# A two-layer-type transformer block pair on one Trainium2 core: both output projections cut into two halves of row blocks, the first half issued inside the attention

## The reference, cut to what matters

```python
# block 1
h = rms_norm(x, attn_pre_g)
q_a, k_a, v_a, q_b, k_b, v_b = split(h @ w_in)
y_a = rms_norm(swa_sink_attention(q_a, k_a, v_a, sinks, slopes), swa_out_g)     # 8 heads of 64, window 128
y_b = diff_attention(q_b, k_b, v_b, lam, slopes, subln_g, lambda_init)          # 4 heads of 2 x 64, values of 128
x = x + rms_norm(concat([y_a, y_b]) @ w_out, attn_post_g)
x = x + rms_norm(conv_ffn(rms_norm(x, ffn_pre_g), w_up, conv_w, conv_b, w_down), ffn_post_g)
# block 2: six modulation vectors from c, as shift, scale and gate
h = modulate(rms_norm(x, g_mix), shift_mix, scale_mix)
q_d, k_d, v_d, q_s, k_s, v_s = split(h @ w_in_2)
mixed = concat([rms_norm(dilated_mixture(q_d, k_d, v_d), g_dil_out),            # 8 heads of 64
                rms_norm(stick_breaking_attention(q_s, k_s, v_s), g_sb_out)])   # 8 heads of 64
x = x + gate_mix * (mixed @ w_out_2)
x = x + gate_ffn * hierarchical_moe(modulate(rms_norm(x, g_ffn), shift_ffn, scale_ffn))  # 32 experts, 2 of them per token
return rms_norm(x, g_final)
```

## Time and profile before

| what | us |
|---|---|
| median of 3 runs (lowest, highest) | 1098.78 (1098.1, 1101.7) |
| profiled execution, its own time | 1095.0 |
| its span, first to last instruction | 1093.2 |
| PE busy | 1016.3 (93%) |
| DVE busy | 538.4 (49%) |
| ACT busy | 330.3 (30%) |
| mean granted clock of TensorE | 0.97 |

### The profile page before, as it was taken

The page is one execution under the profiler, slowest core; times in us unless marked ns, Lnnn a source line. Parts: engine busy times, 40 slices in busy tenths (PEclk is TensorE's granted clock), DMA queues, the critical chain, the costliest instruction groups (busy, mean ns, idle before and its releaser), DMA issues.

```text
span 1093.2 us, 15144 instructions
## 1 busy us (share of the span) xinstructions
PE 1016.3 (93%) x5951; PEld 706.6 (65%) x5951; DVE 538.4 (49%) x901; ACT 330.3 (30%) x507; POOL 75.3 (7%) x109
## 2 busy tenths in 40 slices
PE   6798689999999999999988899999999999999995
PEld 5697569999899998889876444444444444433441
DVE  6756786988989996738674311111111011111113
ACT  4353645445445455527450100000000000000001
POOL 7200010110111110100010000000000000000000
PEclk9899689999999999899989999999999999999998
DMA  7315046778898864244345899799999999999991
GB/s 279 116 40 195 37 155 231 265 275 300 300 330 280 302 242 164 78 160 149 126 170 230 355 425 382 314 384 426 426 425 431 421 426 427 423 426 430 426 401 40
DMA packets 60366, 311.88 MB, mean 285 GB/s; under 512 B 4021, under 2 KB 5386, under 8 KB 47530
## 3 DMA queue, kind: packets, MB, share of 16 engines
q1 hardware_dynamic: 52464, 284.31, 66.1%
q0 software_dynamic: 7456, 26.91, 6.7%
q10 hardware_dynamic: 410, 0.16, 0.1%
HBM read 310.32 MB, written 1.05 MB: 285 GB/s over the span
## 4 chain that ended last, share of the span: by engine, by line
PE 78%; DVE 10%; DMA 5%; ACT 3%; issue 2%; SPq 0%; POOL 0%; DVEq 0%; POOLq 0%; ACTq 0%
PE bank L1134 10%; PE bank L1103 10%; PE bank L744 10%; PE bank L1094 10%; PE bank L745 10%; PE bank L746 10%; PE bank L1045 6%; PE bank L1058 5%; DVE ring_r L1516 5%; DMA ring<-in_w_up 3%; DMA ring<-in_w_in 2%; PE bank L829 1%; PE bank L798 1%; ACT ring_r L1203 1%; DMA final_g<-in_w_ada 1%
## 5 line engine op out<-in xcount | busy, mean ns | idle before, releaser
L744 PE MATMUL bank<-hT_r,ring_r 128*128 128x256 f32 x744 | 217.0, 292 | 11.9 <-DVE ring_r L1516 8.3
L746 PE MATMUL bank<-hT_r,ring_r 128*128 128x256 f32 x744 | 213.8, 287 | 0.0
L1516 DVE TENSOR_TENSOR ring_r<-ring,ring_r 128x2048 fp32r<-128x2048 f32 (+1 forms) x78 | 176.1, 2290 | 21.5 <-ACT ring_r L1203 21.0
L1203 ACT ACTIVATE ring_r<-ring 128x2048 fp32r<-128x2048 f32 (+1 forms) x78 | 144.1, 1891 | 46.0 <-DMA ring<-in_w_up 38.8
L744 PEld LDWEIGHTS bank<-hT_r,ring_r 128*128 128x128 f32 x744 | 146.4, 197 | 15.4 <-issue 9.9
L746 PEld LDWEIGHTS bank<-hT_r,ring_r 128*128 128x128 f32 x744 | 146.2, 197 | 0.0
L745 PE MATMUL bank<-v_tok_r,ring_r 128*128 128x256 f32 x512 | 145.5, 284 | 0.0
L1980 DVE TENSOR_TENSOR scratch<-scratch,bank 128x512 f32<-128x512 f32 x16 | 11.0, 687 | 237.0 <-PE bank L1103 237.0
L1103 PE MATMUL bank<-ring,scratch 128*64 128x512 f32 x496 | 113.3, 595 | 0.0
L1134 PE MATMUL bank<-ring,scratch 128*64 128x512 f32 x480 | 106.3, 595 | 6.6 <-ACT scratch L1417 6.6
L1094 PE MATMUL bank<-ring,scratch 128*64 128x512 f32 x480 | 105.6, 592 | 0.0
(11 more groups left out here) (292 smaller groups left out, 1417.8 us busy)
## 6 DMA issues: line engine op xcount, KB each, us to landing
ring<-in_w_up SPq DMA_DIRECT2D x47, 2048.0 KB, 12.6
ring<-in_w_down SPq DMA_DIRECT2D x37, 2048.0 KB, 10.3
ring<-in_w_gate SPq DMA_DIRECT2D x30, 2048.0 KB, 12.1
ring<-in_w_in SPq DMA_DIRECT2D x9, 2048.0 KB, 8.0
kT<-in_w_ada POOLq DMA_DIRECT2D x24, 512.0 KB, 9.1
ring<-in_w_out SPq DMA_DIRECT2D x4, 2048.0 KB, 8.3
scratch<-in_w_ada POOLq DMA_DIRECT2D x12, 512.0 KB, 6.5
final_g<-in_w_ada POOLq DMA_DIRECT2D x12, 512.0 KB, 7.1
```

Source lines behind the costliest of these rows:

```text
L744: pe.matmul(dst, lhs[0], rhs[0], start=start, stop=False, **flags)
L746: return pe.matmul(dst, lhs[1], rhs[0], start=False, stop=stop, **flags)
L1203: sc.activation(hi, raw, ACT.Copy).then_inc(s_whi, 1)
L1516: last = ve.tensor_tensor(lo, raw, hi, ALU.subtract)
```

## The change

- **First half of each output projection.** The heads that are done first (windowed in block 1, stick-breaking in block 2) fill one half of the concatenated rows: four of the eight row blocks. These rows are now scaled, transposed, split and multiplied during the attention of the other heads: FIRST_HALF gives the steps of PE (transposes in step 9 of block 1 and step 2 of block 2, the four results' first 12 matmuls each in steps 10 to 13 and 4 to 7), PARTS_AT those of ACT and DVE. The results stay in four PSUM banks (PROJ_BANKS), and `rest_of_projection` adds the other four row blocks behind the attention.
- **Splits.** In block 1 the first output chunk is split in steps 7 and 8 instead of 8 and 9, the second in steps 9 and 10 instead of behind the attention.
- **Projection items.** The last ten items of block 1 are ordered so that chunk 2 of w_in is used up earlier: the third and fourth query item come before the first value item.
- **Roots.** Norms of the two halves are asked for separately: two more powers on POOL in each block.
- **First loads.** SP issues chunks 1 and 2 of w_in ahead of the sinks and lambda vectors; ACT splits chunk 2 ahead of lambda's exponential and of its copies, and DVE takes the copies of items 1 and 3 ahead of the split of chunk 2.
- **Small ones.** The norm of the feed-forward part goes to another buffer (rows2), and POOL's first modulation loads wait for the transposes of that norm.

```diff
-        ROOTS += [(5 * t, 5) for t in range(T)]
+        ROOTS += [(5 * t, 1) for t in range(T)]
+        ROOTS += [(5 * t + 1, 4) for t in range(T)]
...
+        TURN_K = {"attn1": (0, KD), "swa": (0, HALF_K), "diff": (HALF_K, KD), "ffn": (0, KD), "attn2": (0, KD),
+                  "sb": (HALF_K, KD), "dil": (0, HALF_K), "moe": (0, KD)}
...
+        PROJ_BANKS = [{(0, 0): 6, (1, 0): 7, (0, 1): 0, (1, 1): 1}, {(0, 0): 4, (1, 0): 5, (0, 1): 0, (1, 1): 1}]
...
-        for pair_of in range(2):
-            for h in (2 * pair_of, 2 * pair_of + 1):
-                items1.append(((QB0 + h * P) // HALF, "q", ("pair", (QB0 + h * P) % HALF, 8 + 2 * h)))
-                items1.append(((KB0 + h * P) // HALF, "k", ((KB0 + h * P) % HALF, 1 + h)))
-            items1.append((3 + pair_of, "v", (S * (1 - pair_of), S, P + S * pair_of)))
...
+        items1 += [q_item(0), k_item(0), q_item(1), k_item(1), q_item(2), q_item(3), v_item(0), k_item(2), k_item(3),
+                   v_item(1)]
...
+        FIRST_HALF = [("swa", {9: None, 10: (0, 0), 11: (1, 0), 12: (0, 1), 13: (1, 1)}),
+                      ("sb", {2: None, 4: (0, 0), 5: (1, 0), 6: (0, 1), 7: (1, 1)})]
+        PARTS_AT = [(9, 10), (2, 3)]
...
-        SPLITS = [{1: (N_IN + 3, 0), 2: (N_IN + 3, 1), 4: (N_IN + 4, 0), 5: (N_IN + 4, 1), 8: (N_OUT, 0),
-                   9: (N_OUT, 1)},
+        SPLITS = [{1: (N_IN + 3, 0), 2: (N_IN + 3, 1), 4: (N_IN + 4, 0), 5: (N_IN + 4, 1), 7: (N_OUT, 0),
+                   8: (N_OUT, 1), 9: (N_OUT + 1, 0), 10: (N_OUT + 1, 1)},
...
+            for c in range(1, LANES):
+                straight(N_IN + c, w_in[:, :, c * HALF:(c + 1) * HALF])
             sp.dma_start(sinks, a["swa_sinks"][0].partition_broadcast(P)).then_inc(s_sink, 16)
             for n, name in enumerate(("diff_lq1", "diff_lk1", "diff_lq2", "diff_lk2")):
                 sp.dma_start(lamv[:, n, :], a[name][0].partition_broadcast(P)).then_inc(s_lamv, 16)
-            for c in range(1, IN_CHUNKS):
+            for c in range(LANES, IN_CHUNKS):
...
+                    tag, steps = FIRST_HALF[blk]
+                    if i in steps and steps[i] is None:
+                        if blk == 0:
+                            piece_taken(blk, len(items1))
+                        turn(tag, mix)
+                    elif i in steps:
+                        t, c = steps[i]
+                        if PROJ_BANKS[blk][t, c] < 2:
+                            pe.wait_ge(s_log[blk], len(units) - 1 + PROJ_BANKS[blk][t, c])
+                        out_projection(blk, tag, t, c, first=True)
+
+            def out_projection(blk, tag, t, c, first):
+                n = (N_OUT, N_OUT2)[blk] + c
+                split_ready(n)
+                w = split_view(n % LANES)
+                ks = range(*TURN_K[tag])
+                for j, k in enumerate(ks):
+                    pe.wait_ge(s_hT[tag], max(place_in_turn(tag, k) + 1, 2))
+                    last = product(PS[PROJ_BANKS[blk][t, c]][:, :], tiles(tag, k, t * P, P), both(w, k, 0, HALF),
+                                   start=(first and j == 0), stop=(not first and k == ks[-1]), skip_group_check=True)
+                return last
+
+            def rest_of_projection(blk, tag):
+                turn(tag, mix)
+                for t in range(T):
+                    for c in range(2):
+                        out_projection(blk, tag, t, c, first=False).then_inc(s_proj[blk], 1)
...
             split(N_IN + 1)
+            split(N_IN + 2)
             sc.wait_ge(s_lamx, 1)
             sc.activation(lam2, lam2, ACT.Exp).then_inc(s_lame, 1)
-            take(0, range(3))
-            split(N_IN + 2)
-            take(0, range(3, AHEAD[0]))
+            take(0, range(AHEAD[0]))
             softmaxes(0, BETWEEN[0], SPLITS[0])
-            split(N_OUT + 1)
-            rounded("mix1", lambda k: vec[:, 2, R_SWA + k:R_SWA + k + 1] if k < 4 else subc)
+            rounded("diff", gain_of_mix[0])
...
+                    if blk == 1 and i in (1, 2):
+                        stick_breaking_scale(i - 1)
+                    if blk == 0 and i - 4 in (ends[("swa", t)] for t in range(T)):
+                        scale_window(units[i - 4]["t"])
+                    if i == PARTS_AT[blk][1]:
+                        low(("swa", "sb")[blk], gain_of_mix[blk])
```

More of the change, by code:

```diff
@@ L834, in attention @@
                         project(blk, n_base, n)
-            def out_projection(blk, n_base):
-                tag = ("mix1", "mix2")[blk]
+                    tag, steps = FIRST_HALF[blk]
[20 more added lines that the diff above has]
+                turn(tag, mix)
                 for t in range(T):
                     for c in range(2):
-                        split_ready(n_base + c)
-                        w = split_view((n_base + c) % LANES)
-                        for k in range(KD):
-                            if t == 0 and c == 0:
-                                pe.wait_ge(s_hT[tag], k + 1)
-                            last = product(PS[4 + 2 * t + c][:, :], tiles(tag, k, t * P, P), both(w, k, 0, HALF),
-                                           start=(k == 0), stop=(k == KD - 1))
-                        last.then_inc(s_proj[blk], 1)
+                        out_projection(blk, tag, t, c, first=False).then_inc(s_proj[blk], 1)
             pe.wait_ge(s_const, 1)
@@ L1501, in low @@
                                 .then_inc(s_shift, 1)
-                    if shift is not None and k > 0:
+                    if shift is not None and k > first:
                         ve.wait_ge(s_shift, k)
-                        ve.tensor_tensor(dst[:, k - 1, :], shifted[:, k - 1, :], hi_T[:, k - 1, :], ALU.subtract)\
+                        ve.tensor_tensor(low_tile(tag, k - 1), shifted[:, k - 1, :], hi_T[:, k - 1, :], ALU.subtract)\
                             .then_inc(s_hT[tag], 1)
@@ L1613, in finish, with scale_window @@
                     ve.wait_ge(s_done[blk], done)
-                    if u["kind"] == "swa":
-                        mean_squares(window, junk[:, 0:HALF], 5 * t)
-                        return
-                    ask_root(mean_squares(window, junk[:, 0:HALF], 2 * t))
-                    root()
-                    for c in range(2):
-                        last = ve.tensor_scalar(mix[:, t, c * HALF:(c + 1) * HALF], mix[:, t, c * HALF:(c + 1) * HALF],
-                                                rstd[:, 2 * t + c:2 * t + c + 1], None, ALU.mult)
-                    last.then_inc(s_src["mix2"], 1)
+                    ask_root(mean_squares(window, junk[:, 0:HALF], column()))
+                    if u["kind"] == "dil":
+                        ve.tensor_scalar(window, window, root(), None, ALU.mult).then_inc(s_src["dil"], 1)
+                def scale_window(t):
+                    window = mix[:, t, 0:HALF]
+                    ve.tensor_scalar(window, window, root(), None, ALU.mult).then_inc(s_src["swa"], 1)
                 logits(0)
@@ L1645, in softmaxes, with post_norm @@
                         split_one(*splits[i - 1])
-            def post_norm(m, rows, t, read=None):
+            def post_norm(m, banks, rows, t, read=None):
                 at = column()
@@ L1655, in post_norm @@
                                                          sq[:, 2 * t + 1:2 * t + 2], ALU.add, ALU.add))
-                    last = ve.tensor_tensor(mix[:, t, half], PS[4 + 2 * t + c][:, :], rows[:, half], ALU.mult)
+                    last = ve.tensor_tensor(mix[:, t, half], PS[banks[t, c]][:, :], rows[:, half], ALU.mult)
                 if read is None:
@@ L1668, in gated @@
                     ve.wait_ge(bank_done, 2 * t + c + 1)
-                    then(ve.tensor_tensor(mix[:, t, half], PS[bank + 2 * t + c][:, :], rows[:, half], ALU.mult))
+                    then(ve.tensor_tensor(mix[:, t, half], PS[banks[t, c]][:, :], rows[:, half], ALU.mult))
                     then(ve.tensor_tensor(x[:, t, half], x[:, t, half], mix[:, t, half], ALU.add))
@@ L1732, in _ @@
             then(ve.tensor_scalar(lam, lam2[:, 0:1], lam2[:, 1:2], LAMBDA_INIT, ALU.subtract, ALU.add))
-            take(0, range(3))
+            take(0, range(AHEAD[0] - 2))
             split(N_IN + 2)
-            take(0, range(3, AHEAD[0] - 1))
             ve.wait_ge(s_const, 7)
             multiplicity()
-            take(0, range(AHEAD[0] - 1, AHEAD[0]))
+            take(0, range(AHEAD[0] - 2, AHEAD[0]))
             ve.wait_ge(s_mask, 1)
             softmaxes(0, BETWEEN[0], SPLITS[0])
-            low("mix1", lambda k: vec[:, 2, R_SWA + k:R_SWA + k + 1] if k < 4 else subc)
-            split(N_OUT + 1)
+            low("diff", gain_of_mix[0])
             ve.tensor_scalar(frac, iota[:, 0:NEXP], 1.0 / 64, None, ALU.mult)
@@ L1886, in _ @@
             ve.memset(ranks[:, :, PASSES * NEXP:], -1.0).then_inc(s_mixed, 1)
-            low("mix2", lambda k: vec[:, 2, R_DIL + k:R_DIL + k + 1])
+            low("dil", gain_of_mix[1])
             ve.wait_ge(s_mod, 6)
```

(2 more changed lines are left out.)

123 lines of the change are left out of this document (76 added, 47 removed).

## The result

| what | before | changed kernel |
|---|---|---|
| median (lowest, highest) of 4 runs, us | 1099.2 (1098.1, 1101.7) | 1088.8 (1085.1, 1091.4) |
| ratio, 95% interval | | 0.9909 (0.9886 to 0.9932) |
| profiled execution, its span | 1095.0, 1093.2 | 1091.4, 1089.8 |
| PE busy in it, us | 1016.3 | 1016.1 |

The account below looks back on a forecast made before the run. PE was taken to bound the kernel (78% of the chain of waits), with DVE full in the first attention from 104. Terms -4.5 + 2.2 + 0.6 = -1.7 took the median from 1098.8 to 1097.1 us, range 1091 to 1103.

Parts of the forecast that it names:

- First loads, -4.5: Start: chunks 1 and 2 ahead of the broadcasts make DVE's copy ahead of the attention 4.5 us earlier, kept up to 104.
- the first scores: Sign at the start of the attention: PE's first scores near 42 instead of 46.45; forecast wrong if at 45 or later.
- rival 2: Start: the gap at 12 to 17.6 is chunk 1's own start, not the broadcasts'; no gain there, 1101.6 us; chance 0.12.
- Items, 0: Projections before 104 us: PE is full, so the new order moves 24 products between steps and adds none.
- First attention, +2.2: From 104 us to the second norm's end: work moved into DVE's full stretch makes the stage 2.2 us longer.
- the last difference: Sign in the first attention: DVE's last difference about 6.5 us later relative to the copy of the last value projection.
- the good end: First attention: PE at full rate throughout, so the stage costs +1.1 us instead of +2.2.
- Second attention, +0.6: Block 2's attention and projection: middle of -0.6 us at the higher clock level and +1.8 at the lower.
- the end at the higher level (-0.6): Second attention with PE's clock at the higher level: end at 595.9 against 596.5, so -0.6 us.
- Rival 1: Start and both attentions: DVE slips between POOL's selects (-6.0), PE stays at the higher level (+1.1, -0.6); 1093.3 us; chance 0.25.
- Rival 3: First attention: PE's clock stays at the lower level through all product groups, +7.5 us on the sum, 1104.6; chance 0.13.
- the norm's end: Sign after the first attention: second norm's end 2 us later relative to the copy of the last value projection.

Follow-up runs that it names:

- e1: Kernel before with the new order of first loads alone (SP's chunks, ACT's and DVE's split of chunk 2): 1093.1 us, ratio 0.9957.
- e8: Kernel before with SP's queue alone in the new order, chunks 1 and 2 ahead of the broadcasts: 1092.6 us, ratio 0.9961.
- e5: Changed kernel with DVE's eight counting operations behind the last two copies of the first items instead of ahead: 1086.9 us, ratio 0.9888.
- e2: Kernel before with the new first loads and the new order of the last ten projection items: 1091.4 us, ratio 0.9938.
- e10: Kernel before with the new order of the last ten projection items alone: 1095.2 us, ratio 0.9980.
- e3: Changed kernel with block 2's output projection as before, without its first half in the attention: 1091.5 us, ratio 0.9943.
- e4: The changed kernel run again, nothing altered: 1089.9 us, ratio 0.9924 against the kernel before.
- e12: Changed kernel with block 1's output projection as before, without its first half in the attention: 1088.8 us, ratio 0.9918.
- e13: Kernel before with PE turning the first token tile again in three waits (2, 4 and 2 times), nothing of the change: 1094.9 us, ratio 0.9969.
- e7: Changed kernel with counting moved later on DVE and PE's repeated transposes ahead of feed-forward and routing: 1082.3 us, ratio 0.9860.
- e6: Changed kernel with PE turning the first tile again 7 times ahead of feed-forward and 3 ahead of routing: 1088.7 us, ratio 0.9913.
- e11: Changed kernel with later counting, repeated transposes, and the modulation's one-column products writing 64 columns: 1080.8 us, ratio 0.9852.

## Why the prediction was wrong, by its own steps

Three steps failed. The items' new order was put at nothing and brought 1.7 to 2.9 us. The first attention was to cost 2.2 and cost 0.2 to 1.1. The second attention was to cost 0.6 and brought 1.6 to 2.6.

**First loads, -4.5: right in size, in part by another path.** -5.3 (e1), -5.5 (e8); the first scores came 4.9 earlier. The broadcasts did hold the queue in front of chunk 1; behind the chunks they are through 2 us after the last one, and DVE waits 0.59 for them, so rival 2 falls. Which operations POOL's selects would catch was wrong: lambda's vectors came at 24.9, not 28, ahead of the selects, the selects came 4.2 later than the prediction left them, and the split of chunk 2 was caught in lambda's place. That the two errors nearly cancel is luck. By the Trainium skill's rule (page "SBUF — State Buffer", section "SBUF: two separate sides") DVE's split and POOL's select exclude each other. The traces agree: the two halves took 7.13 in the changed kernel and 8.34 in e5, against 4.6 when free.

**Items, 0: wrong.** "The new order of the projections moves 24 products from one step to another and adds none." It adds none, but it takes away waits: 1.7 us by e2 less e1, 2.9 by e10 (0.4 to 4.0 by its interval). The window of the earlier trace rows has 18.8 of 20 us and I called that full; of the 1.2 that are missing 0.7 were gain, and the wait of 0.57 at 71.14 is ahead of the window.

**First attention, +2.2: too high.** It is +0.2 (e3 less e2) to +1.1 (e4 less e12) in the time, the small changes of the norm's buffer and of POOL's wait included and neither clear of the scatter; V to N is 51.3 to 51.5 in six of seven profiles with them and 51.2 to 51.7 without. The queue of DVE was right: +6.4 at the last difference, of 6.5. Two sizes failed. PE ran its groups at the higher level, which the prediction had as the good end, and ended 1.1 earlier. The seventh profile, e3, is near the case that was forecast: its first group's products start 0.43 apart, the last value products end 25.3 behind V (24.9 predicted) and V to N is 52.8. And "the 48 products that left PE's tail give nothing here" was wrong by 1.0: without the halves DVE waits for PE and ACT in the second post norm. From the timelines of DVE before and in e2:

```profile
150.77 0.16 DVE L1654 SCALAR_TENSOR_TENSOR small<-small 128x1 f32<-128x1 f32 x1 [1.00 <-ACT final_g L1274]
143.46 0.16 DVE L1657 SCALAR_TENSOR_TENSOR small<-small 128x1 f32<-128x1 f32 x1 [1.01 <-ACT final_g L1278]
```

In the changed kernel the same instruction (143.43, above) waits for nothing. The wait stands in the trace that the prediction was made from; "almost without a wait" hid it.

**Second attention, +0.6: wrong.** -1.6 (e4 less e3) to -2.6 (e12 less e2) in the time, where the intervals overlap; the stage shows it more clearly, 48.8 to 50.3 in the seven profiles with the halves against 50.2 to 53.3 in the eight without. The instants were right: last value products 11 later, scaling's end 0.9 earlier, which is the end at the higher level (-0.6). What failed is the base. D to M was 50.2 in the profile of before, at the low end of the scatter to 53.3: the mean is 51.9 without the halves and 49.3 with them. The old tail idles 2.6 us in front of its products and then often pays for them at half rate; e3's PE, timeline and window, and then the changed kernel's window (columns of the earlier trace rows):

```profile
563.36 1.97 PE L772 MATMUL bank<-ident,mix 128*128 128x128 f32 x8 [2.57 <-DVE mix L1669]
565.98 0.76 PE L783 MATMUL bank<-ring_r,hT_r 128*128 128x512 f32 x1 [0.65 <-DVE bias_r L1548]
564.00:568.00 4.00, 3.35 (x12) 2.59 (x11) 3.04 (x8) 3.02 (x8) 2.02 (x3) 0.50 0.91 311
```

```profile
564.00:568.00 4.00, 4.00 (x26) 3.43 (x25) 0.00 (x0) 0.60 (x1) 0.00 (x0) 1.00 0.01 4
```

With the halves PE is never idle for more than 1.4 us there and the clock is 1.00 from 564 to 588 in all seven; without them a piece at the lower level starts between 561 and 570 in all eight. It is 3.4 us long in before and 6.8 in e3; PE's waits up to it are the same in both (1.28, 0.33, 2.57), and D to M is 50.2 and 52.0. At the experts' entry M to X is 19.9 against 19.0 in the mean of four and seven profiles without turns there, but the four lie between 17.8 and 21.2, so that some 0.9 is given back is not shown. That the clock is the cause is argued from these rows; e13 moved the time but not this stage, so it is not shown.

**Sum and rivals.** Step by step e1, e2, e3 and e4 make -5.3, -1.7, +0.2 and -1.6, in all -8.5 before rounding. They build on each other, so they add up to e4 whatever the terms are; that the terms are independent is not tested. The 10.4 of the first four executions is 1.9 more, inside its interval. Rival 1 was nearest. Its second part happened (PE at the higher level in both attentions), its first did not (DVE did not slip between the selects), and its 5.5 us left out the items and the base. Rival 3 did not happen: the groups' products start 0.23 apart, 0.43 in the first group alone in e3 and, from its fourth product on, in e7. Of the signs, the first scores (41.5 for 42) and the last difference (6.4 for 6.5) held; the norm's end, 2 later by the forecast, was 0.2 earlier. The range was built on one profile's clock, and left its scatter out.

## What to carry to other kernels

A small load that stands in a queue ahead of a large one can cost far more than its bytes: here five of them were worth 5.3 to 5.5 us, and behind the large ones next to nothing. A window that is "full" at 94% can have a gain of up to 6% in it (here 0.7 of 20 us): look for the waits before writing zero. And where the same kernel scatters by several us, find the stretches that scatter in a second profile before a forecast leans on an instant in the first.

## What was not expected of the hardware

- 32 fp32 products with 128 rows of weights take 3.63 us with one column and 3.68 with 64, and behind the first group of one-column ones the granted clock fell to the lower level in 11 of 14 profiles (not in before, e6 and e8), while PE counts as busy throughout. In the one profile with 64 columns it did not fall there; that the columns are the reason is not shown.
- Transposes repeated into a gap of 8.7 us kept the granted clock at 1.00 through it in e6, e7 and e11 (a mean of 0.57 to 0.63 without them in after, e3, e4 and e5). The second tile's transposes behind it then took 1.09, 1.09 and 1.59 us instead of 1.97.
- Behind five partition broadcasts of 256 bytes or less per partition a 2 MB chunk landed 5.3 us later (22.77) than ahead of them (17.43), with the transfers at a share of 0.14 from 12 to 14 and 0.34 from 14 to 16; behind two chunks the broadcasts were through 2 us after them.
- The time of one kernel goes with its mean clock, but loosely: beside e1 to e4 the kernel before had 1093.2 us at 0.972 and 1101.7 at 0.965, while 1098.0 beside e5 was also at 0.972. Over the 84 executions beside the experiments the correlation is -0.6.
